# Two-block model on one core: the recurrence's steps in another written order, values and alpha turned together, w between the transposes of the inverse

## What is computed

```python
z = h @ w_in
y_a = multi_scale_pool(u_a, pool_w, pool_scale)
y_b = rwkv7_time_mix(sh, ...)
y = concatenate([y_a * silu(g_a), y_b * silu(g_b)])
x = x + y @ w_out
return rmsnorm(x, final_gain)
```

```python
sa = einsum('bhvk,bhk->bhv', state, -kk_t)
state = state * w_t + sa[..., None] * (kk_t * a_t) + v_t[..., None] * k_t
y_t = einsum('bhvk,bhk->bhv', state, r_t)
```

## Time and profile before

| | us |
|---|---|
| median of 3 runs | 1608.11 |
| lowest and highest | 1606.2 and 1608.54 |
| the profiled execution's own time | 1610.82 |
| its span, first to last instruction | 1608.1 |
| TensorE busy (matmul) | 1556.8 (97%) |
| VectorE busy | 783.4 (49%) |
| ScalarE busy | 620.1 (39%) |
| GpSimd busy | 527.0 (33%) |

### The profile page before, as it was taken

How to read it: one execution, slowest core, us unless ns; L and a number is a source line. 1 busy time by engine, 2 the same in 40 slices (tenths; PEclk the granted TensorE clock), 3 DMA queues, 4 the chain that set the end, 5 groups by cost and what they waited for, 6 DMA issues and landing times.

```text
span 1608.1 us, 31516 instructions
## 1 busy us (share of the span) xinstructions
PE 1556.8 (97%) x12758; PEld 1388.4 (86%) x12758; DVE 783.4 (49%) x1372; ACT 620.1 (39%) x1142; POOL 527.0 (33%) x235
## 2 busy tenths in 40 slices
PE   8999998999999999999999999999999999998997
PEld 7898987999999999989999788888889876787766
DVE  5444434764132231475446642332315899657655
ACT  5666665453232231342224532322324544433322
POOL 2222222044444444124441344444441244450011
PEclk9999999999999999999999999999999999999998
DMA  5121111222222222223222222222332222200001
GB/s 200 41 67 53 54 55 54 77 93 92 93 93 92 93 93 92 71 75 115 84 90 86 85 93 98 99 92 92 95 102 70 76 92 79 92 17 3 3 27 52
DMA packets 35691, 125.69 MB, mean 78 GB/s; under 512 B 4080, under 2 KB 4336, under 8 KB 35568
## 3 DMA queue, kind: packets, MB, share of 16 engines
q1 hardware_dynamic: 35568, 123.90, 23.6%
HBM read 121.79 MB, written 2.10 MB: 77 GB/s over the span
## 4 chain that ended last, share of the span: by engine, by line
PE 69%; DVE 9%; issue 4%; ACT 2%; POOL 1%; DMA 0%; POOLq 0%; DVEq 0%; ACTq 0%; SPq 0%
PE G L1512 59%; PE G L1847 2%; PE ST L1847 2%; PE PV L1847 1%; PE PO L1847 1%; DVE wlo L949 1%; DVE m L969 1%; POOL wlo L475 1%; PE ST L1478 1%; DVE t L1251 1%; DVE hres L976 1%; DVE acc L1401 0%; DVE z L1236 0%; PE ST L1512 0%; DVE z L1254 0%
## 5 line engine op out<-in xcount | busy, mean ns | idle before, releaser
L475 POOL TENSOR_TENSOR wlo<-raw,whi 128x1024 fp32r<-128x1024 f32 x207 | 501.2, 2423 | 1047.0 <-ACT whi L531 732.5
L1512 PE MATMUL G<-xh,whi 128*128 128x258 f32 (+3 forms) x1504 | 367.2, 307 | 10.2 <-DVE wlo L949 4.1
L1512 PE MATMUL G<-xl,whi 128*128 128x258 f32 (+3 forms) x1504 | 357.6, 300 | 0.0
L1512 PE MATMUL G<-xh,wlo 128*128 128x258 f32 (+3 forms) x1504 | 356.3, 299 | 1.1 <-DVE xl L917 1.1
L1512 PE MATMUL G<-ah,whi 128*128 128x256 f32 (+2 forms) x1024 | 278.0, 312 | 1.9 <-DVE al L1136 1.6
L1512 PE MATMUL G<-ah,wlo 128*128 128x256 f32 (+2 forms) x1024 | 276.3, 310 | 0.0
L1512 PE MATMUL G<-al,whi 128*128 128x256 f32 (+2 forms) x1024 | 276.2, 310 | 0.0
L1512 PEld LDWEIGHTS G<-xh,whi 128*128 128x128 f32 x1504 | 243.0, 189 | 33.8 <-issue 10.5
L1512 PEld LDWEIGHTS G<-xh,wlo 128*128 128x128 f32 x1504 | 244.3, 189 | 10.9 <-DVE xl L917 1.3
L1512 PEld LDWEIGHTS G<-xl,whi 128*128 128x128 f32 x1504 | 243.2, 189 | 9.9
L541 ACT ACTIVATE whi<-raw 128x1024 fp32r<-128x1024 f32 x96 | 101.8, 1061 | 388.3 <-PE G L1512 388.3
(11 more groups left out here) (358 smaller groups left out, 1996.0 us busy)
## 6 DMA issues: line engine op xcount, KB each, us to landing
raw<-weights_dram SPq DMA_DIRECT2D x225, 512.0 KB, 3.7
hres<-xT_dram SPq DMA_DIRECT2D x8, 264.0 KB, 4.9
out_dram<-hres SPq DMA_DIRECT2D x8, 256.0 KB, 2.3
con<-consts_dram SPq DMA_DIRECT2D x1, 512.0 KB, 7.0
mat<-mats_dram SPq DMA_DIRECT2D x1, 512.0 KB, 7.6
con<-consts_dram SPq DMA_DIRECT2D x1, 264.0 KB, 6.3
vec<-vecs_dram SPq DMA_DIRECT2D x1, 171.0 KB, 6.3
con<-consts_dram SPq DMA_DIRECT2D x1, 128.0 KB, 4.0
```

Source lines behind the costliest of these rows:

```text
L475: nc.gpsimd.tensor_tensor(wlo[:, s], raw[:, s % 2], whi[:, s].bitcast(F32), ALU.subtract)\
L1512: last_of[0] = nc.tensor.matmul(to[:, p0:p1], wt[:, w, ws], xt[:, k, t0 - off:t1_ - off], start=k == 0 and q == 0, stop=k == KT - 1 and q ...
```

## The change

The rule of `woven` is replaced by a list of words, one period of the order, in which a word is a step of the system of pair p, of the tail of pair p - 1, of the next pair's `gram` and `lm`, or (`norm4` to `norm6`) of the tail of pair p - 2. `rv` and `at` become one step `turn`, whose products alternate between the two pairs of quadrants; VectorE's sums of `rv` (Ya) go with it. `w` moves into `td`, its products alternating with the transposes. `y3` gets one more wait, on a count that other steps have already waited for in part.

```diff
--- before
+++ after
         START = [("gram", 0), ("gram", 1), ("lm", 0), ("lm", 1)]
-        SYSTEM = [("rv", 0), ("D2", 0), ("D2", 1), ("D4", 0), ("y2", 0), ("D4", 1), ("y2", 1), ("at", 0), ("D8", 0),
-                  ("y3", 0), ("D8", 1), ("y3", 1), ("bk", 0), ("y4", 0), ("y4", 1), ("w", 0), ("td", 0), ("td", 1)]
-        SYSTEM += [(n, g) for n in ("ht", "z1", "z2", "z3") for g in range(2)] + [("q", 0), ("pt", 0)]
-
-        UNDER = {("z2", 1): START[:1], ("z3", 1): START[1:2], ("pt", 0): START[2:]}
-
         CHAIN = [("u", 0)] + [(n, c + d) for c in range(NCH - 1) for n, d in (("s", 0), ("u", 1))]
         TAIL = CHAIN + [("y", 0), ("mu", 0), ("sq", 0), ("var", 0), ("sd", 0)] + [("norm", i) for i in range(7)]
 
-        JOIN = {"u": 4, "s": 4, "mix": 19, "y": 18}
+        MIXES = {"ht1": 0, "z10": 1, "z11": 2, "z20": 3}
+        LATE = ('norm4', 'norm5', 'norm6')
+
+
+        PERIOD = ("u0 D20 D21 D40 norm4 D41 s0 turn0 u1 norm5 D80 y20 D81 s1 norm6 y21 y30 u2 bk0 y31 s2 u3 "
+                  "y40 s3 u4 y41 td0 s4 td1 u5 ht0 s5 ht1 u6 z10 z11 s6 z20 z21 u7 z30 z31 y0 gram0 q0 mu0 "
+                  "sq0 gram1 lm0 pt0 var0 lm1 sd0 norm0 norm1 norm2 norm3").split()
 
         def woven():
 
 
+            tails = {n + str(g): (n, g) for n, g in TAIL}
+            starts = {n + str(g): (n, g) for n, g in START}
             steps = [(system_, 0, *t) for t in START]
-            other = [(mix_, g, "mix", 0) for g in range(4)]
             for p in range(PAIRS):
-                for i, t in enumerate(SYSTEM):
-                    steps.append((system_, p, *t))
-                    if p + 1 < PAIRS:
-                        steps += [(system_, p + 1, *n) for n in UNDER.get(t, ())]
-                    if other and (other[0][1] < p - 1 or i >= JOIN.get(other[0][2], 0)):
-                        steps.append(other.pop(0))
-                other += [(tail_, p, *t) for t in TAIL]
+                for word in PERIOD:
+                    if word in tails:
+                        q = p - 2 if word in LATE else p - 1
+                        if q >= 0:
+                            steps.append((tail_, q, *tails[word]))
+                    elif word in starts:
+                        if p + 1 < PAIRS:
+                            steps.append((system_, p + 1, *starts[word]))
+                    else:
+                        steps.append((system_, p, word[:-1], int(word[-1])))
+                    if p == 0 and word in MIXES:
+                        steps.append((mix_, MIXES[word], "mix", 0))
+            other = [(tail_, PAIRS - 2, *tails[word]) for word in LATE] + [(tail_, PAIRS - 1, *t) for t in TAIL]
             ends, n = [], 0
             for i, t in enumerate(other):
                 ends.append(t)
@@ -828,26 +835,25 @@
 
             def system(p, name, g):
                 n2 = 2 * p + g + 1
-                if name == "rv":
+                if name == "turn":
                     act.wait_ge(S("rv_turned"), p + 1)
                     for x in range(2):
                         nc.scalar.activation(UV[p % 2][x][ROW[1 - x]], chunks(bank(0))[ROW[1 - x]], ACT.Copy)\
                             .then_inc(S("vt_out"), 1)
-                elif name == "at":
                     copy_out("at_turned", p + 1, "at_out", at_, chunks(bank(1)))
                 elif name == "D2":
                     copy_out("d2_ready", n2, "d2_out", PB2[:, g].rearrange("p k c t -> p (k c t)"), bank(2 + g))
                 elif name == "bk":
                     for x in range(2):
                         copy_out("bk_turned", p + 1, "bk_out", BKt[p % 2][x][:], chunks(bank(x)))
-                elif name == "w":
-                    copy_out("w_ready", p + 1, "w_out", Wm, chunks(bank(0)))
                 elif name == "D4":
                     copy_out("d4_ready", n2, "d4_out", PB4[:, g].rearrange("p k c t -> p (k c t)"), bank(2 + g))
                 elif name == "D8":
                     copy_out("d8_ready", n2, "d8_out", B8[:, HALF[g]], chunks(bank(2 + g)[:, 0:4 * CH]))
                 elif name == "td":
                     copy_out("td_ready", n2, "td_out", PB2[:, g, 0], chunks(bank(4 + g)[:, 0:4 * CH]))
+                    if g == 1:
+                        copy_out("w_ready", p + 1, "w_out", Wm, chunks(bank(0)))
                 elif name == "ht":
                     copy_out("ht_ready", n2, "ht_out", B8[:, HALF[g]], chunks(bank(4 + g)[:, 0:4 * CH]))
                 elif name == "q":
@@ -1340,7 +1346,7 @@
                     dve.wait_ge(S("lm_ready"), n2)
                     nc.vector.tensor_tensor(Dm[:, HALF[k]], chunks(bank(4 + k)[:, 0:4 * CH]), mask(C_MD), ALU.mult)\
                         .then_inc(S("D_out"), 1)
-                elif name == "rv":
+                elif name == "turn":
 
                     dve.wait_ge(S("gram_out"), 12 * (p + 1))
                     for x in range(2):
@@ -1924,19 +1930,17 @@
                     if p:
                         pe.wait_ge(S(("q_out", "pt_out")[g]), p)
                     both(at4(4), al, lambda x, c: BK[ROW[x], p, c, x, :], g).then_inc(S("lm_ready"), 1)
-                elif name == "rv":
-
-                    pe.wait_ge(S("gram_out"), 12 * p + 6)
+                elif name == "turn":
+
+                    pe.wait_ge(S("gram_out"), 12 * p + 12)
                     pe.wait_ge(S("bonus_ready"), PAIRS)
-                    for h in halves:
-                        last = both(at8(0, True), lambda x, c: z[ROW[x], 9 + p, 1 + CH * c:1 + CH * c + CH], eye, h)
-                    last.then_inc(S("rv_turned"), 1)
-                elif name == "at":
-
-                    pe.wait_ge(S("gram_out"), 12 * p + 12)
-                    for h in halves:
-                        last = both(at8(1), al, eye, h)
-                    last.then_inc(S("at_turned"), 1)
+                    for c in range(NCH):
+                        for x in range(2):
+                            v = mm(at8(0, True)(x, c), z[ROW[x], 9 + p, 1 + CH * c:1 + CH * c + CH], eye(x, c))
+                        for x in range(2):
+                            a = mm(at8(1)(x, c), al(x, c), eye(x, c))
+                    v.then_inc(S("rv_turned"), 1)
+                    a.then_inc(S("at_turned"), 1)
                 elif name == "D2":
 
                     if p == 0 and g == 0:
@@ -1955,11 +1959,6 @@
                             last = nc.tensor.transpose(bank(x)[:, CH * c:CH * c + CH],
                                                        BK[ROW[x], p, c].rearrange("p k t -> p (k t)"), eye(x, c))
                     last.then_inc(S("bk_turned"), 1)
-                elif name == "w":
-                    pe.wait_ge(S("bk_out"), 2 * p + 1)
-                    for h in halves:
-                        last = both(at8(0), LakT, lambda x, c: UV[p % 2][x][ROW[1 - x], c, :], h)
-                    last.then_inc(S("w_ready"), 1)
                 elif name == "D4":
                     pe.wait_ge(S("d2_out"), n2)
                     both(lambda x, c: bank(2 + g)[ROW[x], CH * (c % 4):CH * (c % 4) + CH], kind_of(PB2, 1), kind_of(PB2, 0), g)
@@ -1973,6 +1972,7 @@
                     pe.wait_ge(S("d4_out"), n2)
                     both(at4(2), kind_of(PB4, 1), kind_of(PB4, 0), g).then_inc(S("d8_ready"), 1)
                 elif name == "y3":
+                    pe.wait_ge(S("d4_out"), n2)
                     pe.wait_ge(S("y2_out"), n2)
                     both(at4(4), kind_of(PB4, 0), of(Yb), g).then_inc(S("y3_ready"), 1)
                 elif name == "y4":
@@ -1981,8 +1981,16 @@
                     both(at4(4), of(B8), of(Ya), g).then_inc(S("y4_ready"), 1)
                 elif name == "td":
 
+                    pe.wait_ge(S("bk_out"), 2 * p + 1)
                     pe.wait_ge(S("y4_out"), n2)
-                    both(at4(4), of(Yb), eye, g).then_inc(S("td_ready"), 1)
+                    for c in range(4 * g, 4 * g + 4):
+                        for x in range(2):
+                            t = mm(at4(4)(x, c), of(Yb)(x, c), eye(x, c))
+                        for x in range(2):
+                            w = mm(at8(0)(x, c), LakT(x, c), UV[p % 2][x][ROW[1 - x], c, :])
+                    t.then_inc(S("td_ready"), 1)
+                    if g == 1:
+                        w.then_inc(S("w_ready"), 1)
                 elif name == "ht":
                     pe.wait_ge(S("td_out"), n2)
                     both(at4(4), of(ET), kind_of(PB2, 0), g).then_inc(S("ht_ready"), 1)
```

## The result

The changed kernel takes 1598.67 us (median of 5 runs, 1596.05 to 1599.27); the kernel before, on the same chip, 1608.53 (5 runs, 1606.2 to 1609.88). The ratio is 0.9933, 95% interval 0.992 to 0.9945: 10.8 us faster, with bounds of 8.8 and 12.9. The forecast was 5.7 us.

The account below looks back on a forecast made before the run. PE was taken to bound the kernel, with gaps (pair 2 busy 29.81 of 33.80 us). Gains 0.65 + 5.06 + 4.17 less 2.88 gave 7.0, less 1.3 for the clock 5.7: from 1608.11 to 1602.4 us, range 1598.5 to 1607.5.

Parts of the forecast that it names:

- Pairs 0, 1 and 2: Recurrence stretches, D2 to D2 of the next pair: forecast gains of 0.65, 5.06 and 4.17 us.
- The wait ahead of q: PE's wait for VectorE's sums (z31, Ya) before q; gram was to cover it, some 0.9 us in pair 0.
- the lower bound of 0.94: Turn's 64 alternating instructions: 0.94 us if each quadrant keeps its own pace; upper bound 1.52, 1.13 taken.
- table load to 7.24, root 7.93, reciprocals to 11.36: End of pair 3, times from z30: a 1.28 us load before the root delays the first low half; 2.88 us lost.
- PE idle 1.4 us ahead of s0 in pairs 2 and 3: Sign that the forecast is right: PE waits 1.4 us before s0 for the copy of U behind late reciprocals.
- var to low half longer by 2.9 us in pair 3: Sign that the forecast is right: in pair 3, var to the output stage's first low half grows by 2.9 us.
- The clock: Output stage: some 3.5 us idle ahead of the first tile halves PE's clock; 1.3 us lost, bounds 0 and 3.07.
- a single precedent: Earlier in the trace, 3.42 us idle up to 1329.06, then clock 0.50 for 6.14 us.
- rival 1: Output stage: the clock does not fall after the idle gap; gain 7.0 us, 1601.1 us; chance 0.24.
- Rival 2: turn and td: alternating groups run no faster than in succession; put at 1606 us; chance 0.16.
- rival 3: Pairs 2 and 3: idle before s0 grows to about 3 us and more, clock falls there; 1612 us; chance 0.07.
- Rival 4: Whole walk: small overlooked waits, a hand-over 0.1 us longer for 50 steps in three pairs, eat the gain; 1608 us; chance 0.05.

Follow-up runs that it names:

- e1: Changed kernel with its new order kept but the alternating groups in turn and td taken apart again; 1601.14 us, ratio 0.9953.
- e3_tables: Changed kernel plus a one-column exponential on ScalarE behind the copy of y in pairs 0 to 2; 1597.07 us, ratio 0.9925.
- e10: The changed kernel again, unedited, for a second profile and a second set of 5 runs; ratio 0.9935 to the kernel before.
- e5: Changed kernel with the next pair's gram moved back to behind z2's second half and behind y0; 1601.2 us, ratio 0.9957.
- e4: Changed kernel with 19 instead of 8 filling matmuls ahead of the output stage's first tile; ratio 0.9929.
- e6: Changed kernel with norm4 to norm6 put directly behind norm3, ahead of the next pair's masks on VectorE; 1605.35 us, ratio 0.9984.
- e7: Changed kernel with norm0 to norm3 of pair 2 moved into the output stage and early output tiles run by rows; 1598.72 us, ratio 0.9947.

## Why the prediction was wrong in size

**What held.** Pairs 0, 1 and 2: forecast 26.32, 27.87 and 29.63, measured 26.42, 27.95 and 29.29. The wait ahead of q is gone, s0 in pair 2 comes 4.88 behind D2 (forecast 5.12), PE idles 0.98 there (forecast 1.37). turn takes 1.00, near the lower bound of 0.94; 1.13 had been taken.

The 64 starts of turn in 1.00 us are 15.6 ns each. By the floor of some 25 ns from start to start that the Trainium skill gives (TensorE: Matmul & The Clock Gate, Part 1, section "Wait — 56ns, not 53.3ns?") they would take an estimated 1.60; this trace does not agree. With 1.74 for the same matmuls in e1 it is their order over the quadrants that decides.

**The step that failed** is "table load to 7.24, root 7.93, reciprocals to 11.36, ... 32.30 against 29.42: 2.88 lost". The stretch was 30.46, so 1.04 was lost, 1.84 less. The one load in the earlier trace rows was taken for a part of every square and root. It stood in pair 1's stretch of both kernels alone: the first root of the recurrence pays it, and with squares, copies and roots only between them the later ones find their table loaded. The profile of the kernel before showed this already. e3_tables puts the load back and gets 1.22 of the 1.84. The remaining 0.6 is the walk's own: in e3 q still comes 0.44 earlier than forecast, and from q to the low half it takes 0.18 less.

The same load was counted ahead of pair 3's s0 too. There PE idled 0.35 instead of some 1.4, the mark of it in the trace that had been named beforehand ("PE idle 1.4 us ahead of s0 in pairs 2 and 3"), half right. Another named mark, var to low half longer by 2.9 us in pair 3, was wrong as it stood: 7.15 us before (1528.15 to 1535.30), 5.18 after. It is D2 to the low half that was forecast longer by that much.

**The clock** was priced at 1.3 by a single precedent. From the first tile to the third s step it takes 11.50 us in the first profile and 11.48 in e1 (clock fallen), 10.44 in e10, 10.43 in e5 and 10.42 in e4 (not fallen). So it costs 1.1, in some executions: behind 2.96 us idle the clock was down when the tile began in two profiles (the changed kernel, e1) and never fell in two (e10, e5). In e3, behind 3.54 us, it fell 1.5 us into the tiles for 3.4 us, and the same distance takes 10.58. Forecast and rival 1 were thus not two theories about the kernel: the same kernel did both. The precedent itself was one of several outcomes: behind its 3.42 us the clock is 0.50 for 6.8 us in the first profile of the kernel before and for 3.4 us in the second (1328.9 to 1332.3). And the argument for rival 1, gaps of up to 0.9 us in pair 2, overlooked the longest, 1.72 us ahead of q at 1501.43, behind which the clock stayed at 1.00 too.

**The sum.** Measured and forecast differ by 5.1 us (10.8 and 5.7). The pair stretches account for 2.1 of it: 1.84 in pair 3, 0.34 in pair 2, and less than 0.2 either way elsewhere. The clock's 1.3 is the next part, where it does not fall. The rest, 1 to 2 us, was not found. With the pair stretches as measured the gain at the low half is 9.07, and it is kept whole where the clock stays up (e10: 140.60 less 131.39 is 9.2) or comes to 8.07 where it falls. Both intervals of the ratio begin below 9.2 (8.8 and 8.2 us), both central values lie 1 to 2 us above it. Whether there is another us outside the recurrence stays open; the profiles' first gram matmuls lie from 1402.05 to 1407.02 over all the kernels, which is more scatter than that.

**What paid.** Not one part of the change. Taking out the mixing costs 3.2 us, the late norms 8.2, gram's place 3.9: 15.3 together, against 10.8 for all, and the mixing by itself, at turn's old place, loses 2.4. Each of the first three is a difference of two ratios, and by their intervals it is uncertain by an estimated 2.5 to 3 us to either side; for the mixing the stretch (3.57) says the same, for the norms the two pair stretches (7.9). They fit an account in which each part removes what would hold up the chain next once the others are done; no run took out two parts at once. Rival 2 (alternation no faster) is refuted by turn's 1.00; rival 3 (the idle ahead of s0 grows to 3 us and the clock falls) did not come, 0.98 and 0.35 us at a clock of 1.00, but e6 shows its mechanism whole in pair 2: s0 7.24 us behind D2, 3.34 idle, the clock down behind it, 3.53 lost. In its pair 3, with 2.71 idle, the clock did not fall. Rival 4 did not come.

## What to carry to other kernels

A duration that shows once in a trace is not yet a price per step: count its rows over the whole stage before multiplying it. When one list orders several engines, ask for each moved step what its VectorE or ScalarE part stands in front of; here the place of three norm steps was worth 8.2 us and the mixed matmuls 3.2. Take parts out of the whole change as well as adding them one at a time: the mixing, which lost 2.4 us alone (at turn's old place), was worth 3.2 in company. And profile the same kernel twice before pricing a fall of the clock.

## What the runs showed of the hardware

- 64 matmuls of 64x64 that alternate over four quadrants begin every 15.6 ns on average (1.00 us for 64); the same ones, two quadrants at a time, every 27 ns (1.74 us for 64). The starts come four together every 58 ns in the first case and two together every 58 ns in the second.
- ScalarE loads its table once (1.28 us) for a run of copies, squares and roots (before, after); after an exponential it loads again, both ways (e3_tables).
- The same 2.96 us of idle time on TensorE halves the granted clock in one execution and leaves it at 1.00 in the next (after, e10_after). Idle times of 3.34 us (e6) and 3.54 us (e3) were followed by a fall, one of 2.71 us (e6) was not. In e5 the clock fell from 1437.5 to 1444.3 though no idle time in the 10 us ahead of it was longer than 0.92 us. After a stall of 4.63 us (e7) the mean clock over 20 us was 0.91.
